# The samples' state updates without TensorE: value rows spread by DMA, multiplied by the key on ScalarE, in a two-layer decoder step on one core

## What is computed

```python
S_new = exp(log_a)[:, None] * S + k[:, None] * v[None, :]   # (DK, DV)
o = q @ S_new                                               # (DV,)
```

## Time and profile before

| | us |
|---|---|
| median of 3 runs | 2576.11 |
| lowest, highest | 2573.31, 2579.16 |
| the profiled execution, its own time | 2575.25 |
| its span in the profile | 2573.3 |
| TensorE busy in it | 2519.4 (98%) |
| VectorE busy | 1506.2 (59%) |
| ScalarE busy | 979.3 (38%) |
| POOL busy | 148.8 (6%) |

### The profile page before, as it was taken

How to read it: one execution, slowest core, us unless ns; L and a number is a source line. 1 busy time by engine, 2 the same in 40 slices (tenths; PEclk the granted TensorE clock), 3 DMA queues, 4 the chain that set the end, 5 groups by cost and what they waited for, 6 DMA issues and landing times.

```text
span 2573.3 us, 59631 instructions
## 1 busy us (share of the span) xinstructions
PE 2519.4 (98%) x25169; PEld 2434.3 (95%) x25169; DVE 1506.2 (59%) x2256; ACT 979.3 (38%) x1103; POOL 148.8 (6%) x195
## 2 busy tenths in 40 slices
PE   7799999999999999999999999999999999999998
PEld 5788789999999999999999999999999999999998
DVE  4474554554455445445548988986754655554654
ACT  3143343333233332332335555455433333333333
POOL 1000241100000000000020010200000000000011
PEclk8999999999999999999999999999999999999999
DMA  9998989898998999998655464655555655555553
GB/s 342 376 348 279 327 279 315 269 322 300 308 311 301 309 307 303 309 307 299 217 178 174 155 187 160 204 156 169 164 180 179 180 180 178 177 180 176 179 178 126
DMA packets 476310, 616.56 MB, mean 240 GB/s; under 512 B 10535, under 2 KB 379525, under 8 KB 471785
## 3 DMA queue, kind: packets, MB, share of 16 engines
q1 hardware_dynamic: 469458, 591.70, 69.7%
q0 software_dynamic: 6720, 22.96, 2.9%
HBM read 602.77 MB, written 13.26 MB: 239 GB/s over the span
## 4 chain that ended last, share of the span: by engine, by line
PE 89%; DVE 4%; DMA 3%; ACT 2%; issue 1%; POOL 0%; SPq 0%; ACTq 0%; DVEq 0%; POOLq 0%
PE ps L924 26%; PE ps L925 25%; PE ps L926 25%; PE pm L1043 5%; DMA wide<-in_w_ada 2%; PE ps L968 1%; PE pm L1025 1%; DVE w_lo L2071 1%; PE pm L1063 1%; ACT w_hi L1547 1%; PE pm L1214 1%; PE ps L1119 1%; DVE z L2645 0%; PE ps L1120 0%; PE ps L1121 0%
## 5 line engine op out<-in xcount | busy, mean ns | idle before, releaser
L2071 DVE TENSOR_TENSOR w_lo<-raw,w_hi 128x1024 fp32r<-128x1024 f32 x708 | 877.8, 1241 | 863.2 <-ACT w_hi L1547 857.3
L1547 ACT ACTIVATE w_hi<-raw 128x1024 fp32r<-128x1024 f32 x696 | 735.3, 1058 | 1228.7 <-PE ps L926 1194.5
L924 PE MATMUL ps<-h_hi,w_hi 128*128 128x264 f32 x3616 | 1047.0, 290 | 6.5 <-DVE h_lo L2500 3.3
L925 PE MATMUL ps<-h_lo,w_hi 128*128 128x264 f32 x3616 | 1030.0, 285 | 0.0
L926 PE MATMUL ps<-h_hi,w_lo 128*128 128x264 f32 x3616 | 1028.7, 284 | 0.0
L924 PEld LDWEIGHTS ps<-h_hi,w_hi 128*128 128x128 f32 x3616 | 682.3, 189 | 26.7 <-issue 17.7
L925 PEld LDWEIGHTS ps<-h_lo,w_hi 128*128 128x128 f32 x3616 | 680.9, 188 | 0.7
L926 PEld LDWEIGHTS ps<-h_hi,w_lo 128*128 128x128 f32 x3616 | 680.8, 188 | 0.0
L924 PE MATMUL ps<-f_hi,w_hi 128*128 128x264 f32 x2048 | 585.5, 286 | 0.0
L925 PE MATMUL ps<-f_lo,w_hi 128*128 128x264 f32 x2048 | 583.9, 285 | 0.0
L926 PE MATMUL ps<-f_hi,w_lo 128*128 128x264 f32 x2048 | 583.2, 285 | 0.0
(11 more groups left out here) (386 smaller groups left out, 1626.7 us busy)
## 6 DMA issues: line engine op xcount, KB each, us to landing
raw<-in_mlp_w_up SPq DMA_DIRECT2D x128, 1024.0 KB, 6.0
raw<-in_mlp_w_down SPq DMA_DIRECT2D x128, 1024.0 KB, 5.4
wide<-in_w_ada SPq DMA_DIRECT2D x104, 1024.0 KB, 9.2
wide_late<-in_w_ada SPq DMA_DIRECT2D x56, 1024.0 KB, 9.9
raw<-in_od_w_in SPq DMA_DIRECT2D x48, 1024.0 KB, 5.2
raw<-in_ev_w_in SPq DMA_DIRECT2D x32, 1024.0 KB, 6.5
araw<-in_w_ada SPq DMA_DIRECT2D x24, 1024.0 KB, 9.7
raw<-in_ev_w_out SPq DMA_DIRECT2D x16, 1024.0 KB, 5.5
```

Of the source, the lines that this page charges most:

```text
L924: nc.tensor.matmul(acc, w_hi[:, slot, cols], xh[:, k, :], start=(k == UK * ends[0]), stop=False)
L925: nc.tensor.matmul(acc, w_hi[:, slot, cols], xl[:, k, :], start=False, stop=False)
L1547: nc.scalar.activation(w_hi[:, u, :], raw[:, p, u, :], ACT.Copy).then_inc(hi_ready, 1)
L2071: nc.vector.tensor_tensor(w_lo[:, p, u, :], raw[:, p, u, :], w_hi[:, u, :].bitcast(F32), ALU.subtract).then_inc(lo_ready, 1)
```

## The change

- The keys are no longer turned, and the outer products on TensorE, `k8`, `kmask` and `own` are gone.
- The values are turned into four strips of rows right behind the products of the first chunk's sum (`s1_psum`), 8 or 4 blocks. ScalarE copies them to `v8`. POOL writes them to a new DRAM tensor `v8_rows` in four DMAs, waits for these, and then reads for each sample its row of 1024 or 512 values into all 128 partitions (`spread`, 0.5 or 0.25 MB). There are three such buffers in group 0 and four in the others; they lie over tiles of the recurrence that are free by then (`vt_from` says from which on they wait until the prompt's outputs are done).
- ScalarE multiplies each spread row in place by the key, a scalar per partition, head by head (`key_values`, four instructions a sample, 96 in all). VectorE's update takes that as its last operand, in place of PSUM.
- VectorE and ScalarE treat samples 0 and 1 in step 0 and sample n+1 in step n. TensorE forms the query products of samples n-1 and n in the odd steps n, and has nothing beside the even ones. There are eight steps in place of nine; in layer 0 one idle step is added behind them.
- POOL's order: in group 0 the rows to DRAM and the first spread stand ahead of the write of the prompt's state, and the two state loads and two more spreads ahead of the load of `pastu` (the pooling rows). Behind each state write of sample b stands the spread of b+3 or b+4, and behind that the state load.

```diff
@@ -134,7 +134,7 @@
 CONV_END = max(n for n, count in CONV_AT.items() if count)
-VTURNS = [0, 6, 10, 14]
+VTURNS = [0, 5, 8, 11]
@@ -282,13 +281,14 @@
 st_more = at("st_more", [P, 2, 1024], F32, o_mw)
-v8s = pair("v8", [64, 2, 256], o_dec)
 kdTs = pair("kdT", [P, NCH, HG * DK], [o + 4096 for o in o_dec])
 s2s = pair("s2", [P, 1024], [o + 4096 for o in o_dec])
 vTs = [at(f"vT{layer}", [P, NCH, (1024, 512)[layer]], F32, o_vT[layer]) for layer in range(2)]
 scores = at("scores", [P, NCH, HG, CH], F32, o_sq)
-kmask = at("kmask", [64, 2, 2, DK], F32, o_sq)
-k8 = at("k8", [64, 2, DK], F32, o_hid)
+v8 = at("v8", [P, 2 * P], F32, o_hid)
+values = [[at(f"values{layer}_{i}", [P, n], F32, o) for i, o in enumerate(offsets)] for layer, n, offsets in
+          ((0, 1024, (o_dec[0], o_vT[0], o_vT[0] + 4096)),
+           (1, 512, (o_dec[1], o_dec[1] + 2048, o_dec[1] + 6144, o_vT[1])))]
 o8_rows = at("o8_rows", [P, 256], F32, o_sq + 2048)
@@ -440,11 +440,11 @@
-HEADS = [dict(layer=0, nv=8, dv=256, q=0, k=4, v=8, bufs=4, sum_banks=(2, 0), end_banks=(1, 2), o_banks=(0, 1, 2, 0),
+HEADS = [dict(layer=0, nv=8, dv=256, q=0, k=4, v=8, bufs=4, vbufs=3, vt_from=1, sum_banks=(2, 0), end_banks=(1, 2), o_banks=(0, 1, 2, 0),
               turns={2: 0, 4: 1, 6: 2}, late=3, qk_groups=4, v_group=4),
-         dict(layer=1, nv=4, dv=128, q=0, k=8, v=16, bufs=4, sum_banks=(2,), end_banks=(1,), o_banks=(2, 0),
+         dict(layer=1, nv=4, dv=128, q=0, k=8, v=16, bufs=4, vbufs=4, vt_from=3, sum_banks=(2,), end_banks=(1,), o_banks=(2, 0),
               turns={6: 0}, late=1, qk_groups=N1 + 6, v_group=N1 + 8),
-         dict(layer=1, nv=4, dv=128, q=4, k=12, v=20, bufs=4, sum_banks=(2,), end_banks=(1,), o_banks=(2, 0),
+         dict(layer=1, nv=4, dv=128, q=4, k=12, v=20, bufs=4, vbufs=4, vt_from=3, sum_banks=(2,), end_banks=(1,), o_banks=(2, 0),
               turns={6: 0}, late=1, qk_groups=N1 + 14, v_group=N1 + 16)]
@@ -495,6 +490,16 @@
+def value_rows(q, b):
+    return values[HEADS[q]["layer"]][b % HEADS[q]["vbufs"]]
+def value_arrivals(q, b):
+    i = b % HEADS[q]["vbufs"]
+    before = sum(len(range(i, NS, HEADS[r]["vbufs"])) for r in range(q) if i < HEADS[r]["vbufs"])
+    return before + b // HEADS[q]["vbufs"] + 1
 def ada_buffer(a, h):
@@ -540,6 +545,8 @@
 y_logs = lnv[:, 0:3 * NS].rearrange("p (c n) -> p c n", n=NS)
+v8_rows = nc.dram_tensor("v8_rows", (3, NS, 1024), F32).ap()
@@ -804,19 +811,37 @@
+def spread(b):
+    pool.dma_start(value_rows(q, b)[:, :], v8_rows[q, b:b + 1, 0:n].broadcast_to([P, n])).then_inc(values_in[b % nv_bufs], 16)
+nv_bufs, from_vt = h["vbufs"], h["vt_from"]
 if q == 0:
     pool.wait_ge(ada_used, 2 * PAIR_STEPS)
     load(0)
     load(1)
     yield
+pool.wait_ge(vtr_ready, VTURNS[q + 1])
+for s in range(4):
+    pool.dma_start(v8_rows[q, :, 0:n].rearrange("b (j s c) -> b j s c", s=4, c=P)[:, :, s, :],
+                   v8[(s + 1) * CP - NS:(s + 1) * CP, 0:h["nv"] // 4 * P].rearrange("b (j c) -> b j c", c=P)
+                   ).then_inc(v8_out, 16)
+pool.wait_ge(v8_out, 64 * (q + 1))
+pool.wait_ge(s2_ready, q + 1)
+for b in range(from_vt):
+    spread(b)
+yield
 pool.wait_ge(o_psum, OPAIRS[q + 1])
 for b in range(2 if q == 0 else 0, nb):
     load(b)
+for b in range(from_vt, nv_bufs):
+    spread(b)
 yield
 for b in range(NS):
     pool.wait_ge(st_ready, NS * q + b + 1)
     pool.dma_start(dst[b, hsl].rearrange("h k v -> k h v"),
                    state(q, b).rearrange("p (h v) -> p h v", h=HG)).then_inc(st_out[b % nb], 16)
+    if b + nv_bufs < NS:
+        spread(b + nv_bufs)
     if 0 <= b - 2 < NS - nb:
@@ -834,7 +859,9 @@
 pool.wait_ge(masks_in, 32)
+next(sample_states)
 prompt_state(0)
+next(sample_states)
 pool.wait_ge(small_out, 16)
@@ -1237,7 +1268,13 @@
 last.then_inc(s1_psum, 1)
-yield
+for j in range(nv):
+    s = CP * (j % 4)
+    last = nc.tensor.matmul(pm[s:s + CP, 1, j // 4 * P:(j // 4 + 1) * P], z[:, zv + j, T - CP:T], ident[:, :],
+                            start=True, stop=True, tile_position=(0, s))
+last.then_inc(vtr_psum, 1)
+yield
+pe.wait_ge(vtr_ready, VTURNS[q + 1])
 for h in range(HG):
@@ -1264,41 +1301,15 @@
-pe.wait_ge(s2_ready, q + 1)
+yield
 pe.wait_ge(o_ready, OPAIRS[q + 1])
-def to_strip(bank, h, at_, src):
-    s = 32 * (h // 2)
-    return nc.tensor.matmul(pm[s:s + 32, bank, at_:at_ + P], z[:, src, T - 32:T], ident[:, :],
-                            start=True, stop=True, tile_position=(0, s))
-for i in range(2):
-    for h in (i, 2 + i):
-        last = to_strip(1, h, i * DK, zk + h)
-last.then_inc(vtr_psum, 1)
-for i in range(2):
-    for m in range(dv // P):
-        for h in (i, 2 + i):
-            last = to_strip(2, h, i * dv + m * P, zv + h * dv // P + m)
-last.then_inc(vtr_psum, 1)
-yield
-pe.wait_ge(vtr_ready, VTURNS[q + 1])
 pe.wait_ge(q_ready, q + 1)
-for b in range(NS + 1):
-    if b < NS:
-        pe.wait_ge(kmask_ready, NS * q + b + 1)
-        if b:
-            pe.wait_ge(st_ready, NS * q + b)
-        for i in range(2):
-            for h in (i, 2 + i):
-                s = 32 * (h // 2)
-                last = nc.tensor.matmul(kv_bank(q, h), kmask[s:s + 32, b % 2, i, :], v8[s:s + 32, i, 0:dv],
-                                        start=True, stop=True, tile_position=(s, 0))
-        last.then_inc(kv_psum, 1)
-    if b:
-        pe.wait_ge(st_ready, NS * q + b)
+for n in range(NS):
+    for b in (n - 1, n) if n % 2 else ():
+        pe.wait_ge(st_ready, NS * q + b + 1)
         for h in range(HG):
-            last = nc.tensor.matmul(pm[h * CP:(h + 1) * CP, 2, 0:dv], q_own[:, h, (b - 1) * CP:b * CP],
-                                    state(q, b - 1)[:, h * dv:(h + 1) * dv], start=(b == 1), stop=(b == NS),
+            last = nc.tensor.matmul(pm[h * CP:(h + 1) * CP, 2, 0:dv], q_own[:, h, b * CP:(b + 1) * CP],
+                                    state(q, b)[:, h * dv:(h + 1) * dv], start=(b == 0), stop=(b == NS - 1),
                                     tile_position=(0, h * CP))
@@ -1313,7 +1324,7 @@
-yield
+yield from idle(2)
 pe.wait_ge(o8_taken, 1)
@@ -1709,6 +1720,8 @@
 last.then_inc(s1_ready, 1)
+act.wait_ge(vtr_psum, VTURNS[q + 1])
+nc.scalar.activation(v8[:, 0:nv // 4 * P], pm[:, 1, 0:nv // 4 * P], ACT.Copy).then_inc(vtr_ready, 1)
 yield
@@ -1717,28 +1730,19 @@
-def mask_keys(b):
-    if b >= NS:
-        return
-    if b >= 2:
-        act.wait_ge(kv_psum, NS * q + b - 1)
-    nc.scalar.activation(kmask[:, b % 2, :, :], k8[:, :, :], ACT.Copy,
-                         scale=own[0:64, b:b + 1]).then_inc(kmask_ready, 1)
-act.wait_ge(vtr_psum, VTURNS[q + 1] - 1)
-nc.scalar.activation(k8[:, :, :], pm[0:64, 1, 0:2 * DK].rearrange("p (i n) -> p i n", i=2),
-                     ACT.Copy).then_inc(vtr_ready, 1)
-act.wait_ge(vtr_psum, VTURNS[q + 1])
-act.wait_ge(s2_ready, q + 1)
-nc.scalar.activation(v8[:, :, 0:hd["dv"]], pm[0:64, 2, 0:2 * hd["dv"]].rearrange("p (i n) -> p i n", i=2),
-                     ACT.Copy).then_inc(vtr_ready, 1)
-act.wait_ge(own_ready, 1)
-act.wait_ge(vtr_ready, VTURNS[q + 1] - 1)
-mask_keys(0)
-mask_keys(1)
-yield
-for b in range(NS + 1):
-    mask_keys(b + 2)
+def key_values(b):
+    act.wait_ge(values_in[b % hd["vbufs"]], 16 * value_arrivals(q, b))
+    for h in range(HG):
+        v_ = value_rows(q, b)[:, h * dv:(h + 1) * dv]
+        last = nc.scalar.activation(v_, v_, ACT.Copy, scale=z[:, zk + h, TP + b:TP + b + 1])
+    last.then_inc(values_ready, 1)
+yield
+for n in range(NS):
+    if n < NS - 1:
+        key_values(n + (n > 0))
+    if n == 0:
+        key_values(1)
     yield
@@ -2477,16 +2479,18 @@
 dve.wait_ge(dec8_ready, q + 1)
-for b in range(NS):
-    dve.wait_ge(kv_psum, NS * q + b + 1)
-    dve.wait_ge(st_in[b % hd["bufs"]], 16 * transfers(q, b))
-    for h in range(HG):
-        o = h * dv
-        s_ = state(q, b)[:, o:o + dv]
-        last = nc.vector.scalar_tensor_tensor(s_, s_, decay8[:, h, b:b + 1],
-                                              kv_bank(q, h), ALU.mult, ALU.add)
-    last.then_inc(st_ready, 1)
-    yield
+for n in range(NS):
+    for b in (0, 1) if n == 0 else (n + 1,) if n < NS - 1 else ():
+        dve.wait_ge(values_ready, NS * q + b + 1)
+        dve.wait_ge(st_in[b % hd["bufs"]], 16 * transfers(q, b))
+        for h in range(HG):
+            o = h * dv
+            s_ = state(q, b)[:, o:o + dv]
+            last = nc.vector.scalar_tensor_tensor(s_, s_, decay8[:, h, b:b + 1],
+                                                  value_rows(q, b)[:, o:o + dv], ALU.mult, ALU.add)
+        last.then_inc(st_ready, 1)
+    if n < NS - 1:
+        yield
 dve.wait_ge(o8_psum, NS * (q + 1))
```

More of the change, by code:

```diff
@@ L205, in build @@
         skipped = sb("skipped", [P, 2])
-        own = sb("own", [P, NS])
         o_rs = arena(2 * T * 4)
@@ L383, in build @@
         dec8_ready = sem("dec8_ready")
-        kmask_ready = sem("kmask_ready")
-        kv_psum = sem("kv_psum")
+        v8_out = sem("v8_out")
+        values_in = [sem(f"values_in{i}") for i in range(4)]
+        values_ready = sem("values_ready")
```

(8 more changed lines are left out.)

12 lines of the change are left out of this document (3 added, 9 removed).

## The result

The changed kernel takes 2591.57 us (median of 5, 2587.85 to 2593.83) against 2576.44 us before (median of 5, 2573.31 to 2579.24): ratio 1.0055, 95% interval 1.0043 to 1.0068. It is **slower by 15 us**, 0.55%, where the forecast was no change. The profiled execution took 2591.57 us, span 2589.4.

The account below looks back on a forecast made before the run. TensorE, busy 98% of the span, was taken to bound the kernel, with DMA at 91% in group 0's stage. Group 0 +8, group 1 -3 and group 2 -5 summed to 0: 2576 us, range 2563 to 2592.

Parts of the forecast that it names:

- the bytes as the bound of group 0: Group 0: DMA engines need 55 us for POOL's 10.5 MB and 8.4 MB of weights, making state 7 ready at 313.
- the state loads of layer 1: Groups 1 and 2: loads used a step earlier, mostly covered by a 3 us lead; cost 0.3 to 0.7 us.
- Group 0, forecast +8: Layer 0's sample updates: TensorE passes the same point at 317.4 instead of 309.2, 8 us later.
- Group 1, forecast -3: Layer 1's first group: ScalarE's chain starts 2.2 us earlier, runs 1.2 longer; 3 of 6.7 us saved.
- Group 2, forecast -5: Layer 1's second group: no ScalarE chain, 6.7 us nearly given; 5 us saved after loads and VectorE.
- VectorE's lag: Group 2: 1 us taken off the saving for VectorE running behind.
- three restarts: Group 0: three fewer TensorE restarts after side work, 3 x 0.19 = 0.6 us saved.
- Spread landing 10 us or more: Group 0, between 257 and 317: expected sign, a spread lands 10 us or more after issue.
- TensorE waiting 15 us or more: Group 0: expected sign, TensorE waits at the odd steps for states, 15 us or more in all.
- Slow spreads: Rival, group 0's queue: reading one row 128 times costs twice per MB, group 0 loses 19 us; 2587 us, chance 0.20.
- Layer 1 gives nothing: Rival, groups 1 and 2: ScalarE's added work and busy VectorE leave no gain, group 0 +8; 2584 us, chance 0.14.
- Mostly hidden: Rival, group 0: idle DMA time, cheaper long rows or lagging weights hide the transfers; 2561 to 2568 us, chance 0.29.

Follow-up runs that it names:

- e10: Changed kernel with later state loads one sample earlier, a fourth value buffer in group 0 and pooling rows loaded after the last sample; 2575.45 us, ratio 0.9997.
- e4: Changed kernel with POOL issuing each later state load one sample earlier; 2578.43 us, ratio 1.0012.
- e2: Changed kernel with each spread carrying only the first head's quarter of the value row, so other heads' values are left out; 2583.72 us, ratio 1.0038.
- e12: Changed kernel with a fourth value buffer in group 0 and pooling rows loaded after the last sample, state loads as late as in the change; 2585.10 us.
- e5: Layer 1 as in the changed kernel, layer 0 with the code of the kernel before; 2576.61 us, ratio 1.0002.
- e8: Layer 0 as in the kernel before, layer 1 as changed with each later state load one sample earlier; 2573.39 us, ratio 0.9992.
- e1: Changed kernel with unused idle products on TensorE ahead of waits for states in all three groups; 2583.76 us, ratio 1.0032.
- e9: Layer 0 as before, layer 1 changed with state loads a sample earlier, plus 34 idle products ahead of sample 5 in group 1; 2572.55 us, ratio 0.9986.
- e11: Changed kernel with earlier state loads, fourth value buffer, late pooling rows, and idle products ahead of sample 5 in groups 0 and 1; 2575.53 us, ratio 0.9995.
- e6: Changed kernel with each spread reading 128 different weight rows instead of one row 128 times, leaving out the samples' outer products; 2586.10 us, ratio 1.0044.

## Why the prediction was wrong

Three terms of the sum failed: the bytes as the bound of group 0, the state loads of layer 1 at 0.3 to 0.7 us, and the granted clock, which stands in it at nothing. That the time lies inside the range, at its very end, is luck: the range reaches that far only for spreads at twice the price, which did not come.

**Group 0, forecast +8, measured +11.2.** The size is near, the reason is not. The step "the engines need 10.5 x 2.94 + 8.4 x 2.88 = 55 us" took the bytes for the bound. e10 moves 9.95 MB on POOL's queue (the 10.5 without the pooling rows) and 8.02 of weights in the 47 us up to 304, at 55.2% x 47 / 9.95 = 2.61 and 46.7% x 47 / 8.02 = 2.74 us a MB, and costs 1.8 us. So the two prices of the earlier trace rows were too high for a full queue; with those of e10 the same sum is 10.5 x 2.61 + 8.4 x 2.74 = 50 us, and the forecast for the group would have been an estimated +3. And the weights yield more than was granted them. The page HBM Reference of the Trainium skill (first table), which the prediction weighed, gives about 358 GB/s a core, and its text below the table says that a core which streams alone measures well above this share. This kernel runs on one core and moved 383 in these 47 us: the trace agrees with the text, and the table's figure is no ceiling here. What bound the change is the order of its transfers: sample 3's spread waits for a value buffer that update 0 releases (12 us from issue to use in e4), and then the state loads of samples 4 to 7 are issued a step too late for products that now come up to a step earlier (load 7 at 299.90; in e4, brought to the same start of the stage, 3.3 us sooner). Bytes have a share, by lengthening the landings: 4.3 us for 2.75 MB in e2, 3.2 us of waiting for gate weights in e4, and whatever of the pooling rows' 0.5 MB is in the gain of e10 and e12. Of the two late transfers the prediction saw the state loads in layer 1 only, and the spread that waits for its buffer not at all; it wrote "the queue serves in order" and summed the queue, but did not follow one buffer through it.

**State loads in layer 1, forecast 0.3 to 0.7 us.** It was worked out with a landing of 4.7 us; the load in the chain took 8.65 in group 1 and 6.97 in group 2. In group 2 this is the term most mis-sized: earlier loads give back 2.4 us in e4, and 4.1 between e5 and e8. In group 1 they give back 1.3 us in e4 and nothing between e5 and e8, as ScalarE's chain ends only 1.0 us earlier than the load. (The sum itself slips: 3 x 0.75 + 4.7 + 1 is 8.0 us and not 8.5, which would have made the term smaller still.)

**The granted clock, not in the sum.** Every part of the prediction let TensorE go on at full pace behind a stall, as the earlier trace rows have it for the 2.0 us stall of the kernel before. In the changed kernel the four stretches at the samples with the clock at 0.50 hold 5.76 + 6.34 + 5.67 + 5.66 = 23.4 us of products, which is up to 11.7 us lost. With TensorE kept busy 2.4, 3.0 and 1.1 us come back, 6.5 in all (e1); in group 1 that is most of the 4.6 us by which the stage missed. The page TensorE: Matmul & The Clock Gate of the Trainium skill ("HAM oscillation") describes just this, a wait for DMA behind which TensorE starts at the lower clock, and counts the loss as half the slow time, which gives an estimate of 17 us for these 34 us. The trace agrees on the fall and bounds the loss lower, since TensorE stood still in part of them.

**Group 1, forecast -3.** Its ScalarE chain was the right bound (e8), and in the changed kernel it ends only 1.0 us before the load lands: it starts 1.5 us earlier (forecast 2.2; 1516.43, and e8 was 1.75 us ahead at this stage, against 1519.70) and is 2.1 us longer (forecast 1.2); two blocks of 1.17 us and not 1.0 are 0.3 us of the 0.9 between these, the rest was not taken apart. With loads and clock mended the stage gains 1.5 us (e9), half of the forecast.

**Group 2, forecast -5.** At best -1.7 and -1.9 (e8, e11). VectorE's lag was put at 1 us; in e8 TensorE waits for it four times, 4.2 us in all, 1.2 at most, and the 3.2 us above the forecast are about what is missing.

**What held.** Multiplications of 256 columns take 0.495 us for 0.4 forecast alone and 1.7 for four, 1.6 forecast; updates stay at 0.48 us. The query products' three restarts and the products removed show between the stalls: at 276 of the kernel before, behind the products of samples 0 and 1 and ahead of the first long stall, the main products of the changed kernel are 0.3 us early, although its run began 2.5 us late and the turned rows had cost 0.7. "Spread landing 10 us or more" and "TensorE waiting 15 us or more" hold (11.9 and 16.3).

**The rivals.** Slow spreads: refuted, by 2.67 us a MB and by e6; the time they would have given, 2587, was nearer than mine for another reason. Layer 1 gives nothing: this came true, +2.8 for -8, and in part as it was told: ScalarE's multiplications stand in the chain that holds group 1 as soon as the loads come earlier (e8), and VectorE's lag costs group 2. The state loads and the clock, which it did not name, are the larger part. Mostly hidden: its reason, that weights may lag, is what e10 shows, in a kernel whose order lets it act. The forecast named no mechanism that would cost all three groups at once; the clock and the late load do.

**Slips in the sums.** With group 0 between -5 and 0 and layer 1 at -8, mostly hidden makes -8 to -13, not -15, and slow spreads decide from 4.3 us a MB on, not 4.35. Neither bears on the forecast.

**Open.** Kernels with layer 0 changed lose another 0.4 to 1.3 us between 344 and 1340, those with layer 0 as before do not. The end behind the last main product is 1.3 us shorter in the changed kernel than in the one before. Neither was looked into.

## What to carry to other kernels

When an operand moves from TensorE to a transfer, follow each buffer around its ring (release, issue, landing, use) with the landings of the crowded stretch, not with the median of the whole span; here two such rings in series cost up to 9.4 of 11.2 us, and the bytes that were added cost little once they were mended. Price a new TensorE stall with what the clock takes behind it: the stalls of 3.3 to 7.1 us here were followed by 3.4 to 10.3 us at half clock. And when a change saves in one stage and loses in another, try it in the stages apart: layer 1 alone, with loads a sample earlier and one stall filled with idle products, is the only version that beats the kernel before, by 0.14%.

## What the runs showed of the hardware

The granted clock fell to 0.50 behind each of the stalls of 3.3 to 7.1 us named here (6.9, 4.5 and 3.3 in the changed kernel, 7.1 in e4, 5.0 in e8, 4.8 in e10). Behind shorter ones it did so sometimes, and their length does not tell when: the 2.0 us of the kernel before in group 1 left it at 1.00, a wait of 2.1 us in group 2 of e9 did not; waits of 1.2 us left it at 1.00 in group 2 of e8, and one of 1.2 us at the same place of e10 had 3.4 us at 0.50 behind it; the 1.8 us near 1700 left it at 1.00 in the kernel before and not in the changed one. Products at half pace took 0.22 us and not 0.12 to 0.13. Products whose result nobody reads keep it up, and that pays only where nothing else sets the time of the next wait: 1.0 to 3.0 us in group 1 (e11, e9, e1), nothing in group 0 of e11. One row read by 128 partitions costs what 128 rows cost (11.9 and 11.1 us to landing). With both queues full the 16 engines moved 383 GB/s over 47 us.
